# Attention: the division by the softmax sum after the values product, and masks added by VectorE in the instruction that finds the row maximum

## The chip, the cores and the metric

One core of one Trainium2 chip runs the whole program. The metric is the device time of one execution in microseconds; the time before is the median of three runs.

## The reference, cut to what matters

The program is a stack of four blocks on 512 tokens of width 1024: two "hybrid" layers, one "even" and one "odd" layer, all in float32. Most of the work is gated feed-forward matmuls. The change touches the softmax attention of three of the layers. In a hybrid layer two mixers use it, each with four heads:

```python
# mixer D (mla): plain causal attention, 4 heads, 96-dim keys, 64-dim values
logits = einsum('bthd,bshd->bhts', qb, k) * scale
logits = where(causal, logits, -inf)
p = softmax(logits, axis=-1)
out = einsum('bhts,bshd->bthd', p, v)

# mixer A (dsa): the same over the top-k keys that an indexer picks, 4 heads, 64-dim,
# with a bias by distance; unpicked keys do not count
logits = einsum('bthd,btkhd->bthk', qb, ks) * scale + bias
p = softmax(where(valid, logits, -inf), axis=-1)
out = einsum('bthk,btkhd->bthd', p, vs)
```

The even layer has 8 heads of 64 dimensions (kind E). Its three dilated branches are merged: the kernel adds ln(how many branches see this key) to the scores, with -1e30 where none does, and takes one softmax. So each of the kinds A and E has an added matrix over all its keys, while D needs one only on the diagonal block.

## The kernel before, in words

The program is written by hand, engine by engine, with counted semaphores; each engine runs its queue in program order. Activations live in SBUF with features on partitions and 512 tokens along the free axis. The eight PSUM banks hold 128x512 float32 each. Large matmuls run in three products of rounded halves (`split_product`: w_hi with hi, w_lo with hi, w_hi with lo). A weight tile of 128x1024 (a "unit") is loaded by SyncE into one of four slots; ScalarE writes `w_hi` (`split_unit`, L1379) and VectorE, sometimes GpSimd, writes `w_lo` (L1787).

Attention is a software pipeline over 32 units (`pe_attention` L1029, `act_attention` L1516, `dve_attention` L1966; `pool_attention` L2404 for A). A unit is one head and one block of 128 queries, and sees (tb + 1) x 128 keys, tb from 0 to 3. A hybrid layer does the 16 D units and then the 16 A units; the even layer 32 E units. In iteration i:

- TensorE makes the scores of unit i in one of four banks (0, 1, 4, 5): query times key (L1043, L1044), and the mask as a further matmul, identity times mask, into the same bank (L1045). For D the mask covers only the last 128 columns; for A and E it covers all keys. Then it transposes the probabilities of unit i-2, block by block (L1052, banks 2 and 3), and multiplies the values of unit i-3 (L1063): the values (128 keys x 64) are the weights, the transposed probabilities stream, and the result (64 x 128, features on partitions) lands where it belongs in bank 6 or 7, which gathers 8 units, a pair of heads.
- VectorE finds the negated maximum of unit i (L1974), takes the reciprocal of the sum of unit i-1 (L1982), multiplies the probabilities of i-1 by it (L1985), and copies the transposed probabilities of i-2 to SBUF (L1992).
- ScalarE takes the exponential of unit i from PSUM, with the maximum as bias and the sum as accumulator (L1527, two instructions). When 8 units are done it copies the gathered bank to `xn_hi` and `y` (L1533, L1534).
- For A, GpSimd adds the bias by distance to the index mask (L2413) into one of three tiles, for the mask matmul.

Beside this pipeline, ScalarE and VectorE prepare the output projection: ScalarE splits four units in iterations 12 to 15, VectorE in 15 to 18 and makes `xn_lo` tiles in 8 to 11, 13, 21 and 29. The projection `pe_out` (L858) follows directly on TensorE; `down_bank(m)` is bank (m + 6) % 8. `pe_norm` (L791) and `pe_post` (L1235) form means of squares for the norms, with separate semaphores.

Of the kernel before, what the change touches and what calls it, by code (L numbers as in the profile page):

```python
# [244 lines left out]
NORMS_POST = 3 * DEPTH + 1  # L245
Z_STAGES = [STAGES["in", _l] for _l in range(DEPTH)]
# [26 lines left out]
def program(nc, I, out):  # L273
    ctx = ExitStack()
    with ctx:
# [59 lines left out]
        def T(n):  # L335
            return arena[:, n, :]
# [37 lines left out]

        def score(tb):
            return scores[:, sc_at[tb]:sc_at[tb] + (tb + 1) * P]
# [57 lines left out]
        sq_done = sem("sq_done", 24)  # L434
        norm_ps = sem("norm_ps", 3)
        norm_ln = sem("norm_ln", 3)
        norm_r = sem("norm_r", 3)
# [72 lines left out]
        att_p = sem("att_p", 32)  # L510
# [43 lines left out]
        rsq = sem("rsq")  # L554
        rn_ps = sem("rn_ps")
        rn_ln = sem("rn_ln")
        rn_r = sem("rn_r")
# [233 lines left out]
        def pe_norm(pe, n):  # L791

            for k in range(KD):
                pe.e.wait_ge(sq_done.h, n * KD + (k + 1))
# [63 lines left out]
        def pe_out(pe, st, order, free):  # L858

            for n, k in enumerate(order):  # L860
# [4 lines left out]
                else:  # L865
                    for m in (0, 2, 3, 4, 5, 6, 7, 1):
# [162 lines left out]
        def pe_attention(pe, units, ops):  # L1029

            U = len(units)
            for i in range(U + 3):
                if i < U:
                    ops["ready"](pe, i)
                    m, h, tb = units[i]
                    if i >= 4:
                        pe.e.wait_ge(att_exp.h, att_exp.by(pe.l, i - 3))
                    s = pb[(0, 1, 4, 5)[i % 4]]
                    N = (tb + 1) * P
                    q, k = ops["qk"](m, h)  # L1040
# [14 lines left out]
                if i >= 3:  # L1055
# [17 lines left out]
        def hyb_mask(m, h, tb, u):  # L1073
            if m == "D":
                return C("causal"), tb * P
# [1423 lines left out]
```

## Time and profile before

| | us |
|---|---|
| median of 3 runs (3715.59 to 3719.69) | 3717.46 |
| profiled execution | 3722.82 |
| its span in the trace | 3721.0 |
| TensorE busy | 3533.9 (95%) |
| VectorE busy | 1606.5 (43%) |
| ScalarE busy | 1119.2 (30%) |
| GpSimd busy | 321.9 (9%) |

The span is the time from the first to the last instruction that the hardware profiler recorded. The chain of waits is followed back from the last instruction: each piece is what held up the next one. In a chain row the columns are start and length in microseconds, then engine, tile, line, and how many instructions. A float32 matmul appears as two instructions, a transpose as one. PE is TensorE's matmuls, PEld its weight loads, DVE is VectorE, ACT ScalarE, POOL GpSimd. In a timeline row the brackets hold how long the engine stood idle before the row, and what ended it.

### The profile page before, as it was taken

The page shows a single profiled execution, that of the slowest core. Times are in us where ns is not written, and L with a number is a line of the kernel's source. Part 1 is how long each engine was busy: PE and PEld are TensorE (multiplying, and loading weights), DVE is VectorE, ACT ScalarE, POOL GpSimd, SP SyncE. Part 2 cuts the span into 40 slices and gives each one's busy share as a digit, 9 for nine tenths or more (in the row PEclk, how much of TensorE's full clock was granted, in tenths as well). Part 3 has the DMA queues.
Part 4 walks back from the last instruction along what each step waited for, and adds up shares of the span by engine and source line. Part 5 has one row for each costly group of instructions (what it writes and reads, how often), then busy time and mean ns, then how long its engine had stood idle before and what let it go on. Part 6 is the DMA issues. An engine that isn't in the chain of part 4 may idle for free.

```text
span 3721.0 us, 39381 instructions
## 1 busy us (share of the span) xinstructions
PE 3533.9 (95%) x14540; PEld 2624.5 (71%) x14540; DVE 1606.5 (43%) x2252; ACT 1119.2 (30%) x1631; POOL 321.9 (9%) x180
## 2 busy tenths in 40 slices
PE   8999998999999999999899999889999998889998
PEld 5888663668887888766467888556678886568886
DVE  3332388543323332258654332734443327363322
ACT  3222334332223222234323221212232214432222
POOL 0000133100000000033210000401000002300000
PEclk9999997899999999999699999899999999899999
DMA  4332320023332333322002332331123322223332
GB/s 130 94 96 93 77 74 30 1 60 93 96 94 78 93 96 95 85 69 70 0 29 79 96 96 90 91 72 46 46 73 95 91 90 70 69 65 91 96 96 68
DMA packets 419543, 285.96 MB, mean 77 GB/s; under 512 B 57352, under 2 KB 395116, under 8 KB 419308
## 3 DMA queue, kind: packets, MB, share of 16 engines
q1 hardware_dynamic: 418624, 283.62, 26.2%
q8 instruction: 57, 0.93, 0.1%
q10 hardware_dynamic: 828, 1.13, 0.1%
q14 instruction: 34, 0.28, 0.0%
HBM read 280.24 MB, written 4.47 MB: 77 GB/s over the span
## 4 chain that ended last, share of the span: by engine, by line
PE 87%; DVE 8%; ACT 2%; issue 1%; DMA 1%; SPq 0%; POOL 0%; POOLq 0%; DVEq 0%; ACTq 0%
PE bank L800 24%; PE bank L801 23%; PE bank L802 23%; PE bank L1150 2%; PE bank L1063 1%; PE bank L795 1%; PE bank L1044 1%; PE bank L1045 1%; DVE xn_lo L1782 1%; DVE xn L1772 1%; PE bank L1144 1%; DVE arena L1881 1%; PE bank L1052 1%; DVE arena L1860 1%; DVE small L1857 1%
## 5 line engine op out<-in xcount | busy, mean ns | idle before, releaser
L802 PE MATMUL bank<-xn_lo,w_hi 128*128 128x512 f32 x2800 | 1102.1, 394 | 0.0
L800 PE MATMUL bank<-xn_hi,w_hi 128*128 128x512 f32 x2496 | 1002.2, 402 | 53.6 <-DVE xn_lo L1782 51.3
L801 PE MATMUL bank<-xn_hi,w_lo 128*128 128x512 f32 x2496 | 992.3, 398 | 0.0
L1787 DVE TENSOR_TENSOR w_lo<-wring,w_hi 128x1024 fp32r<-128x1024 f32 x434 | 537.0, 1239 | 1012.7 <-ACT w_hi L1379 995.6
L1379 ACT ACTIVATE w_hi<-wring 128x1024 fp32r<-128x1024 f32 x490 | 514.6, 1052 | 578.4 <-DMA wring<-in_ffn_down 330.2
L802 PEld LDWEIGHTS bank<-xn_lo,w_hi 128*128 128x128 f32 x2800 | 531.5, 190 | 133.5
L800 PEld LDWEIGHTS bank<-xn_hi,w_hi 128*128 128x128 f32 x2496 | 471.1, 189 | 188.8 <-issue 54.3
L801 PEld LDWEIGHTS bank<-xn_hi,w_lo 128*128 128x128 f32 x2496 | 473.3, 190 | 100.1
L801 PE MATMUL bank<-h_hi,w_lo 128*128 (+1 forms) x1056 | 419.6, 397 | 0.0
L802 PE MATMUL bank<-h_lo,w_hi 128*128 (+1 forms) x1056 | 416.5, 394 | 0.0
L800 PE MATMUL bank<-h_hi,w_hi 128*128 (+1 forms) x1056 | 415.4, 393 | 0.0
L1395 ACT ACTIVATE h_hi<-arena x132 | 83.5, 633 | 662.4 <-DVE arena L1801 662.4
L1801 DVE TENSOR_TENSOR arena<-bank,arena 128x512 f32 x132 | 91.4, 692 | 375.5 <-PE bank L802 375.5
L800 PEld LDWEIGHTS bank<-h_hi,w_hi 128*128 128x128 f32 x1056 | 198.2, 188 | 50.2
L801 PEld LDWEIGHTS bank<-h_hi,w_lo 128*128 128x128 f32 x1056 | 198.2, 188 | 47.6
L802 PEld LDWEIGHTS bank<-h_lo,w_hi 128*128 128x128 f32 x1056 | 198.2, 188 | 46.7
L2371 POOL TENSOR_TENSOR w_lo<-wring,w_hi 128x1024 fp32r<-128x1024 f32 x56 | 135.1, 2414 | 1024.8 <-ACT w_hi L1379 1024.8
L1391 ACT ACTIVATE arena<-bank 128x512 f32<-128x512 f32 x132 | 79.2, 600 | 383.9 <-PE bank L802 383.9
L1804 DVE TENSOR_TENSOR h_lo<-arena,h_hi x132 | 91.4, 693 | 134.0 <-ACT h_hi L1395 134.0
L800 PE MATMUL bank<-z_hi,w_hi 128*128 128x512 f32 (+1 forms) x304 | 127.4, 419 | 9.6 <-DVE xn_lo L1782 9.6
L801 PE MATMUL bank<-z_hi,w_lo 128*128 128x512 f32 (+1 forms) x304 | 123.3, 406 | 0.0
L1881 DVE SCALAR_TENSOR_TENSOR arena<-hpad,cur_dw,arena 128x512 f32<-128x512 f32 x120 | 111.2, 991 | 0.0
(360 smaller groups left out, 2998.4 us busy)
## 6 DMA issues: line engine op xcount, KB each, us to landing
wring<-in_ffn_gate SPq DMA_DIRECT2D x88, 512.0 KB, 3.7
wring<-in_ffn_up SPq DMA_DIRECT2D x88, 512.0 KB, 3.7
wring<-in_ffn_down SPq DMA_DIRECT2D x88, 512.0 KB, 3.5
wring<-in_ffn_w_gate SPq DMA_DIRECT2D x44, 512.0 KB, 3.7
wring<-in_ffn_w_up SPq DMA_DIRECT2D x44, 512.0 KB, 3.7
wring<-in_ffn_w_down SPq DMA_DIRECT2D x44, 512.0 KB, 3.5
wring<-in_w_in SPq DMA_DIRECT2D x34, 512.0 KB, 3.6
wring<-in_w_out SPq DMA_DIRECT2D x16, 512.0 KB, 4.9
```

The source lines that it names most:

```text
L800: nc.tensor.matmul(ps, w_hi[:, slot, t, 0:M], hi, start=start, stop=False)
L801: nc.tensor.matmul(ps, w_lo[:, slot, t, 0:M], hi, start=False, stop=False)
L802: return nc.tensor.matmul(ps, w_hi[:, slot, t, 0:M], lo, start=False, stop=stop)
L1150: mm = nc.tensor.matmul(bank[:, :], w[:, k, c * P:(c + 1) * P], xn[:, k, :], start=(k == 0), stop=(k == KD - 1))
L1379: nc.scalar.activation(w_hi[:, slot, :, :].rearrange("p k c -> p (k c)"), wunit[:, slot, :], ACT.Copy).then_inc(u_hi.h, 1)
L1391: nc.scalar.activation(sg[:, c, :], pb[c][:, :], ACT.Silu).then_inc(sg_ready.h, 1)
L1395: nc.scalar.activation(h_hi[:, bass.ds(2 * i + c, 1), :].rearrange("p a c -> p (a c)"), arena[:, bass.ds(2 * i + (H_LO + c), 1), :].rearra ...
L1787: nc.vector.tensor_tensor(w_lo[:, slot, :, :].rearrange("p k c -> p (k c)"), wunit[:, slot, :], w_hi[:, slot, :, :].rearrange("p k c -> p ...
L1801: nc.vector.tensor_tensor(h, pb[2 + c][:, :], sg[:, c, :], ALU.mult).then_inc(h_full.h, 1)
L1804: nc.vector.tensor_tensor(lo, h, hi.bitcast(F32), ALU.subtract).then_inc(h_lo_ready.h, 1)
L1881: ins = nc.vector.scalar_tensor_tensor(out=T(t_hc[ct]), in0=src, scalar=w, in1=T(t_hc[ct]), op0=ALU.mult, op1=ALU.add)
L2371: nc.gpsimd.tensor_tensor(w_lo[:, q, :, :].rearrange("p k c -> p (k c)"), wunit[:, q, :], w_hi[:, q, :, :].rearrange("p k c -> p (k c)").b ...
```

## The change

Four things change in the attention pipeline.

1. A and E: no mask matmul. VectorE reads scores and mask and writes -(scores + mask) to the probability tile, while it keeps the minimum, in one instruction; ScalarE takes exp(-x + that minimum) in place. D keeps its causal mask on TensorE and its plain reduce.
2. The multiply of the probabilities by the reciprocal is gone. The values product is turned round (transposed probabilities as weights, 64 columns of values stream), so that queries lie on partitions, and ScalarE multiplies the 128x64 result by the reciprocal on its way to SBUF (`o_buf`). The results of 8 units are then transposed, four blocks, into bank 5, from which the two copies are made.
3. Banks: scores use three (0, 1, 4); outputs alternate between 6 and 7 by unit; 5 is for the new transposes. The projection's first unit visits the banks in another order and waits for the scalings of the last two units and, for bank 5, the last copy.
4. The semaphores of `pe_norm` and `pe_post` are merged; `pe_mean` serves both.

```diff
@@ pe_attention
-            for i in range(U + 3):
+            for i in range(U + 6):
...
-                    if i >= 4:
-                        pe.e.wait_ge(att_exp.h, att_exp.by(pe.l, i - 3))
-                    s = pb[(0, 1, 4, 5)[i % 4]]
+                    if i >= 3:
+                        taken = att_exp if units[i - 3][0] == "D" else att_max
+                        pe.e.wait_ge(taken.h, taken.by(pe.l, i - 2))
+                    s = pb[(0, 1, 4)[i % 3]]
...
-                    msk, lo = ops["mask"](m, h, tb, i)
+                    lo = tb * P if m == "D" else N
                     if lo:
-                        nc.tensor.matmul(s[:, 0:lo], q[:, tb * P:N], k[:, 0:lo], start=True, stop=True)
-                    nc.tensor.matmul(s[:, lo:N], q[:, tb * P:N], k[:, lo:N], start=True, stop=False)
-                    nc.tensor.matmul(s[:, lo:N], ident, msk, start=False, stop=True).then_inc(att_s.h, 1)
+                        mm = nc.tensor.matmul(s[:, 0:lo], q[:, tb * P:N], k[:, 0:lo], start=True, stop=True)
+                    if lo < N:
+                        nc.tensor.matmul(s[:, lo:N], q[:, tb * P:N], k[:, lo:N], start=True, stop=False)
+                        mm = nc.tensor.matmul(s[:, lo:N], ident, C("causal"), start=False, stop=True)
+                    mm.then_inc(att_s.h, 1)
...
-                    pe.e.wait_ge(att_p.h, att_p.by(pe.l, u + 1))
+                    pe.e.wait_ge(att_exp.h, att_exp.by(pe.l, u + 1))
...
-                    if u % 8 == 0 and u >= 16:
-                        pe.e.wait_ge(y_att.h, y_att.by(pe.l, u // 8 - 1))
-                    o = pb[6 + (u // 8) % 2][64 * (h % 2):64 * (h % 2) + 64, tb * P:(tb + 1) * P]
+                    if u >= 2:
+                        pe.e.wait_ge(att_on.h, att_on.by(pe.l, u - 1))
+                    a = tb * P + 64 * (h % 2)
                     for b in range(tb + 1):
-                        mm = nc.tensor.matmul(o, ops["v"](m, h, b), pt_buf(units, u)[:, b * P:(b + 1) * P],
+                        mm = nc.tensor.matmul(pb[6 + u % 2][:, a:a + 64], pt_buf(units, u)[:, b * P:(b + 1) * P], ops["v"](m, h, b),
                                               start=(b == 0), stop=(b == tb))
                     mm.then_inc(att_o.h, 1)
+                u = i - 5
+                if u >= 0 and u % 8 == 7:
+                    p = u // 8
+                    pe.e.wait_ge(att_on.h, att_on.by(pe.l, u + 1))
+                    if p >= 1:
+                        pe.e.wait_ge(y_att.h, y_att.by(pe.l, p))
+                    for tb in range(TB):
+                        mm = nc.tensor.transpose(pb[5][:, tb * P:(tb + 1) * P], o_buf(units, p)[:, tb * P:(tb + 1) * P], ident)
+                    mm.then_inc(att_y.h, 1)
@@ pe_out
-                    for m in (0, 2, 3, 4, 5, 6, 7, 1):
+                    for m in (2, 3, 4, 5, 6, 0, 1, 7):
@@ att_free
             if m < 2:
-                pe.e.wait_ge(y_att.h, y_att.by(pe.l, 3 + m))
+                pe.e.wait_ge(att_on.h, att_on.by(pe.l, 31 + m))
+            elif m == 7:
+                pe.e.wait_ge(y_att.h, y_att.by(pe.l, 4))
@@ act_attention
-                    if i >= 3:
-                        act.e.wait_ge(att_t.h, att_t.by(act.l, i - 2))
...
+                    if units[i][0] == "D":
+                        if i >= 3:
+                            act.e.wait_ge(att_t.h, att_t.by(act.l, i - 2))
+                        nc.scalar.activation(p, pb[(0, 1, 4)[i % 3]][:, 0:N], ACT.Exp,
+                                             bias=nmax[:, c:c + 1], accum_out=psum_[:, c:c + 1]).then_inc(att_exp.h, 1)
+                    else:
+                        nc.scalar.activation(p, p, ACT.Exp, scale=-1.0,
+                                             bias=nmax[:, c:c + 1], accum_out=psum_[:, c:c + 1]).then_inc(att_exp.h, 1)
                 u = i - 4
+                if 0 <= u < U:
+                    _, h, tb = units[u]
+                    p = u // 8
+                    if p >= 2 and u % 8 == 0:
+                        act.e.wait_ge(att_y.h, att_y.by(act.l, p - 1))
+                    act.e.wait_ge(att_rs.h, att_rs.by(act.l, u + 1))
+                    act.e.wait_ge(att_o.h, att_o.by(act.l, u + 1))
+                    a = tb * P + 64 * (h % 2)
+                    nc.scalar.activation(o_buf(units, p)[:, a:a + 64], pb[6 + u % 2][:, a:a + 64], ACT.Identity,
+                                         scale=rsum[:, u % 4:u % 4 + 1]).then_inc(att_on.h, 1)
+                u = i - 6
                 if u >= 0 and u % 8 == 7:
-                    act.e.wait_ge(att_o.h, att_o.by(act.l, u + 1))
-                    o = pb[6 + (u // 8) % 2][:, :]
+                    act.e.wait_ge(att_y.h, att_y.by(act.l, u // 8 + 1))
+                    o = pb[5][:, :]
@@ dve_attention
+                    if m == "D":
+                        nc.vector.tensor_reduce(nmax[:, c:c + 1], s, AX.X, ALU.max, negate=True).then_inc(att_max.h, 1)
+                    else:
+                        added = mask(dve, h, tb, i)
+                        if i >= 3:
+                            dve.e.wait_ge(att_t.h, att_t.by(dve.l, i - 2))
+                        nc.vector.tensor_tensor_reduce(p_buf(units, i)[:, 0:N], s, added, -1.0, -SENTINEL,
+                                                       ALU.add, ALU.min, nmax[:, c:c + 1]).then_inc(att_max.h, 1)
...
-                        dve.e.wait_ge(att_p.h, att_p.by(dve.l, u - 3))
+                        dve.e.wait_ge(att_on.h, att_on.by(dve.l, u - 3))
                     nc.vector.reciprocal(rsum[:, c:c + 1], psum_[:, c:c + 1]).then_inc(att_rs.h, 1)
-                    p = p_buf(units, u)[:, 0:(units[u][2] + 1) * P]
-                    dve.e.wait_ge(att_rs.h, att_rs.by(dve.l, u + 1))
-                    nc.vector.tensor_scalar(p, p, rsum[:, c:c + 1], None, ALU.mult).then_inc(att_p.h, 1)
...
-                if i in (13, 21, 29):
-                    n = 4 + (i - 13) // 8
+                if i in (15, 23, 31):
+                    n = 4 + (i - 15) // 8
@@ pool_attention
-                    pool.e.wait_ge(att_s.h, att_s.by(pool.l, BM[n - 3] + 1))
+                    pool.e.wait_ge(att_max.h, att_max.by(pool.l, BM[n - 3] + 1))
```

## Rows read from the trace of the kernel before

**Rows 1.** Page, part 1: busy us (share of the span), instructions.

```profile
PE 3533.9 (95%) x14540; PEld 2624.5 (71%) x14540; DVE 1606.5 (43%) x2252; ACT 1119.2 (30%) x1631; POOL 321.9 (9%) x180
```

**Rows 2.** Chain (start, duration, what): one head of the even stage.

```profile
2606.06 0.36 PE bank L1063 x2
...
2606.84 0.42 PE bank L1045 x2
2607.26 0.45 PE bank L1052 x3
...
2612.57 1.02 PE bank L1063 x8
...
2614.64 1.06 PE bank L1045 x2
...
2615.91 0.36 PE bank L1063 x2
```

**Rows 3.** Chain of waits, kind A heads of layer 1: two multiplies.

```profile
734.14 0.74 DVE arena L1985
...
744.29 0.74 DVE arena L1985
```

**Rows 4.** Chain of waits, one D head of layer 1.

```profile
697.04 0.43 DVE arena L1985
...
699.28 0.22 PE bank L1045 x2
...
705.06 0.43 DVE arena L1985
```

**Rows 5.** Timeline (start, duration, instruction, [idle before]): D, then E head.

```profile
704.27 0.69 DVE L1974 TENSOR_REDUCE small<-bank 128x1 f32<-128x512 f32 x1 [0.60 <-PE bank L1045]
...
704.99 0.69 ACT L1527 ACTIVATE arena<-bank,small 128x512 f32<-128x512 f32 x1 [1.88 <-DVE small L1974]
...
705.54 0.31 PEld L1052 LDWEIGHTS bank<-cst,arena 128*128 128x128 f32 x3 [0.28 <-DVE arena L1985]
...
705.58 0.19 ACT L1527 ACTIVATION_READ_ACCUMULATOR arena<-bank,small 128x1 f32 x1
...
2615.73 0.69 DVE L1974 TENSOR_REDUCE small<-bank 128x1 f32<-128x512 f32 x1 [2.02 <-PE bank L1045]
...
2617.00 0.55 PE L1052 MATMUL bank<-cst,arena 128*128 128x128 f32 x3
```

**Rows 6.** Timeline, then ns min/median/max of weight loads (L1063 old values product).

```profile
2423.00 1.89 PE L1185 MATMUL bank<-arena,s_wv 128*128 128x64 f32 x16
...
2424.73 1.51 PE L1150 MATMUL bank<-xn,wring 128*128 128x512 f32 x3
...
L1185 PEld LDWEIGHTS bank<-arena,s_wv x64: 190/192/192, 2422.6 to 2452.2; 128*128 128x128 f32 x64
...
L1063 PEld LDWEIGHTS bank<-arena x480: 132/137/137, 688.3 to 2639.9; 128*64 128x64 f32 x160
```

**Rows 7.** Groups by shape: xcount | busy us, mean ns | idle before.

```profile
L1538 ACT ACTIVATE xn_hi<-xn 128x512 fp32r<-128x512 f32 x12 | 7.4, 619 | 0.0
...
L1533 ACT ACTIVATE xn_hi<-bank 128x512 fp32r<-128x512 f32 x12 | 7.1, 591 | 10.2 <-PE bank L1063 10.2
...
L1527 ACT ACTIVATE arena<-bank,small 128x128 f32<-128x128 f32 x24 | 8.9, 369 | 4.4 <-DVE small L1974 4.4
```

**Rows 8.** Page part 5, timeline, chain: head with weight splits, layer 1.

```profile
L1787 DVE TENSOR_TENSOR w_lo<-wring,w_hi 128x1024 fp32r<-128x1024 f32 x434 | 537.0, 1239 | 1012.7 <-ACT w_hi L1379 995.6
...
713.56 0.55 PE L1052 MATMUL bank<-cst,arena 128*128 128x128 f32 x3
...
724.77 0.55 PE bank L1052 x3
```

**Rows 9.** Chain of waits, end of layer 1's attention.

```profile
756.64 1.87 PE bank L1063 x14
758.51 0.44 PE bank L800
```

More of the change, by code:

```diff
@@ L245, with turn, post_turn @@
 NORMS_POST = 3 * DEPTH + 1
+def turn(n):
+    return n + max(0, n - 3 * DEPTH)
+def post_turn(m):
+    return 3 * DEPTH + 1 + 2 * m
 Z_STAGES = [STAGES["in", _l] for _l in range(DEPTH)]
@@ L373, in pt_buf, with o_buf @@
             return T(((19, 22) if units is HYB_UNITS else (37, 39))[u % 2])
+        def o_buf(units, p):
+            return T(((17, 18) if units is HYB_UNITS else (18, 19))[p % 2])
         def score(tb):
@@ L433, in program @@
         x_ready = sem("x_ready", 24)
[L434 to L437, printed above, removed]
+        sq_done = sem("sq_done")
+        norm_ps = sem("norm_ps")
+        norm_ln = sem("norm_ln")
+        norm_r = sem("norm_r")
         xn_ready = sem("xn_ready", 24)
@@ L509, in program @@
         att_rs = sem("att_rs", 32)
-        att_p = sem("att_p", 32)
+        att_on = sem("att_on", 32)
+        att_y = sem("att_y", 4)
         att_t = sem("att_t", 32)
@@ L1071, in hyb_qk, with hyb_mask, even_mask @@
             return T(t_aq[h // 2])[r:r + 64, :], T(t_ak[h // 2])[r:r + 64, :]
-        def hyb_mask(m, h, tb, u):
-            if m == "D":
-                return C("causal"), tb * P
+        def hyb_mask(dve, h, tb, u):
             if tb == 0:
-                return bias[:, h, SEQ - P:SEQ], 0
-            return T(t_bm[BM.index(u) % 3])[:, 0:(tb + 1) * P], 0
+                dve.e.wait_ge(pro_sb.h, 4 + 2 + A_HEADS)
+                return bias[:, h, SEQ - P:SEQ]
+            dve.e.wait_ge(att_bm.h, att_bm.by(dve.l, BM.index(u) + 1))
+            return T(t_bm[BM.index(u) % 3])[:, 0:(tb + 1) * P]
+        def even_mask(dve, h, tb, u):
+            return C("lnmult")[:, SEQ - (tb + 1) * P:]
         def hyb_v(m, h, b):
@@ L1121, in even_ready @@
                 eng.e.wait_ge(ez_sb.h, len(E_Z))
-        EVEN = dict(qk=even_qk, mask=lambda m, h, tb, u: (C("lnmult")[:, SEQ - (tb + 1) * P:], 0),
-                    v=lambda m, h, b: e_vv[:, b, h * E_DIM:(h + 1) * E_DIM], ready=even_ready)
+        EVEN = dict(qk=even_qk, v=lambda m, h, b: e_vv[:, b, h * E_DIM:(h + 1) * E_DIM], ready=even_ready)
         def pe_even(pe, norms):
@@ L1233, in pe_even @@
                 mm.then_inc((w_used if c else glu_ps).h, 1)
-        def pe_post(pe, m):
-            for k in range(KD):
-                pe.e.wait_ge(rsq.h, m * KD + k + 1)
-                mm = nc.tensor.matmul(pb[6][:, :], C("mean1024"), T(SQ + k), start=(k == 0), stop=(k == KD - 1))
-            mm.then_inc(rn_ps.h, 1)
         def pe_odd(pe):
@@ L1519, in act_attention @@
             U = len(units)
-            for i in range(U + 4):
+            for i in range(U + 6):
                 if i < U:
@@ L1964, in dve_mixers, with dve_attention @@
                                                in1=T(t_or[pr]), op0=ALU.mult, op1=ALU.mult).then_inc(o_n.h, 1)
-        def dve_attention(dve, units, st, order):
+        def dve_attention(dve, units, st, order, mask):
             U = len(units)
@@ L2340, in _ @@
                 dve_mixers(dve)
-                dve_attention(dve, HYB_UNITS, STAGES["out", l], Y_HYB)
+                dve_attention(dve, HYB_UNITS, STAGES["out", l], Y_HYB, hyb_mask)
                 dve_take(dve, STAGES["out", l], add)
@@ L2350, in _ @@
             dve_even(dve)
-            dve_attention(dve, E_UNITS, STAGES["out", "even"], Y_EVEN)
+            dve_attention(dve, E_UNITS, STAGES["out", "even"], Y_EVEN, even_mask)
             dve_take(dve, STAGES["out", "even"], to_r)
```

64 lines of the change are left out of this document (28 added, 36 removed).

## The prediction

> **What bounds the kernel now.** I read the page's busy table first: TensorE is busy 95% of the span, VectorE 43% [rows 1]. That is an average, so I then followed the chain of waits through the three attention stages the change touches (layer 1 from 682 to 758 us, layer 2 the same, the "even" one from 2560 to 2640). A stage has 32 units, one for each head and block of 128 queries; four units (128, 256, 384, 512 keys) make a head and the pattern repeats. In the even stage the chain of one head is TensorE and nothing else: it repeats after 2615.91 - 2606.06 = 9.85 us, four mask matmuls take 0.42 for 128 columns to 1.06 for 512, 0.21 more for each 128, so 0.42 + 0.63 + 0.84 + 1.06 = 2.95, and no wait is in it [rows 2]. Heads of kind A (layers) look alike but repeat after 744.29 - 734.14 = 10.15 us: once a head TensorE waits for the normalised probabilities, whose multiply takes 0.74 there, beside GpSimd's bias addition, where a D head shows 0.43 [rows 3, 4]. Heads of kind D repeat after 705.06 - 697.04 = 8.02 us, of which TensorE waits 0.28 for that multiply [rows 4, 5]. So TensorE is the bound and VectorE ends a wait once a head.
>
> **Sum's base.** The profiled execution took 3722.82 us (span 3721.0 plus 1.82 around it), 5.36 above the median 3717.46 of the three runs shown. Terms are worked out on the former and moved to the median.
>
> **1. Masks leave TensorE (A and E heads, 8 each; D keeps its causal mask).** Removed per head: 2.95 us [rows 2]. Not all is streaming: the mask of 128 columns costs 0.42 in an E head and 0.22 in a D head [rows 2, 4], same shape. What differs is the weights before it: 64 partitions deep in E, 96 in D. So in E a pause of 0.20 stands ahead of each mask. After the change the transposes stand behind that 64-deep matmul and probably inherit the pause. Between 0 and 0.20 for each unit comes back; I take 0.15, nearer to the mask's row because it is the same switch: +0.60 per head.
>
> **2. The values product turns round.** Weights were 64 columns of values with 128 columns of probabilities streaming; now 128 columns of transposed probabilities are weights and 64 columns stream. The state-space stage has this form: 16 such instructions from 2423.00 until the next group at 2424.73, 0.108 each [rows 6]. The old form costs (1.02 - 0.36)/6 = 0.11 each, from 8 against 2 instructions [rows 2]. So the body costs nothing more. Each group's first load stands behind a wait and is longer (190 against 137 ns by the weight-load rows [rows 6]): +0.05 a unit, +0.20 per head, all 24 heads.
>
> **3. Division after the product.** The multiply by the reciprocal (0.43 for 384 columns [rows 4]) leaves VectorE and the path from exponential to transposes. In its place ScalarE scales 128x64 out of PSUM for each unit. That form isn't in the trace; ScalarE's shortest instruction, the accumulator read of one column, takes 0.19, and its exponential of 128 columns 0.37 [rows 5, 7]: between these two, I take 0.30, as it has a scale per partition like the latter.
>
> What is late next: the product of unit u waits until unit u-2 has been scaled, since only two banks take turns. ScalarE takes the scaling of unit i-4 in order, behind the exponential of unit i. So the product of the 256-key unit waits for: widest maximum, widest exponential, accumulator read, scaling. In a D head, from the start of the widest maximum: 0.69 + 0.04 + 0.78 (exponential and its read, 704.99 to 705.77) + 0.30 + 0.05 = 1.86 us [rows 5]. TensorE would be there, without the present wait of 0.28, after 705.54 - 704.27 - 0.28 + 0.44 (transposing; 3 blocks as in rows 2) = 1.43 [rows 5]. It waits 0.43 instead of 0.28. D heads: +0.15 + 0.20 = +0.35, times 8 = +2.8 us.
>
> **4. The fused add, scale and minimum.** It replaces the reduce (0.69 at 512 columns). The trace has no such instruction. Below: the plain reduce, 0.69. Above: two full passes, 1.38. The other two-tensor form beside it, the w_lo subtraction, takes 1.24 for 1024 columns, so one pass for 512 would be under 0.7 [rows 8]. I take 0.75: one PSUM and one SBUF stream, like the reduce in length, with a little for the written tile. The exponential then reads SBUF; the same 512-column copy costs 619 ns from SBUF against 591 from PSUM [rows 7], so +0.03.
>
> The Trainium skill (VectorE: DVE Perf Modes, section "Two Vector instructions with no wait between them") says that an operation which also writes out its accumulator is two instructions. No VectorE row here shows such a pair; ScalarE's exponential does show one, 0.19 us [rows 5]. If it held, each A or E head would wait about 0.15 more (the length of a reciprocal), 2.4 us in all. The skill's same page gives ScalarE 52 cycles more for an SBUF source than for PSUM; the two copy rows show 28 ns, and the measurement decides.
>
> **A and E heads together.** From the start of the widest maximum (2615.73) to the next transposes (2617.00) TensorE needs 1.27, less a mask of 0.42, plus two pauses of 0.15, plus 0.44 for three transposes, plus 0.05: 1.64 [rows 2, 5]. The new chain: 0.75 + 0.04 + 0.81 + 0.30 + 0.05 = 1.95. Wait 0.31. Head: 9.85 - 2.95 + 0.60 + 0.20 + 0.31 = 8.01. E: 8 x (9.85 - 8.01) = 14.7 saved. A: GpSimd's addition no longer meets a multiply, so the same 8.01: 8 x (10.15 - 8.01) = 17.1 saved. Together -31.8. GpSimd must have each bias tile ready for VectorE; it works 4 units ahead on three tiles, about 3 us a head, so nothing.
>
> **5. New transposes.** Outputs now lie queries-first and are transposed back, four blocks for each pair of heads: 4 a stage. In the loop 9 times, 0.44 and a pause of 0.15: +5.4. The last of a stage stands before the output projection: TensorE waits for the last scaling (0.20 until the matmul's end is seen, 0.30, 0.05), then 0.44: about 1.0, three times: +3.0. Before, the projection followed the last product with no gap [rows 9]. The changed bank order there keeps it from waiting further: banks 0 to 4, 6 and 7 come first, 7 x 0.7 us, against two ScalarE copies of 0.6 for bank 5.
>
> **6. The stretch with weight splitting.** In four units VectorE also makes a w_lo (1.24 us) [rows 8]. New load: (0.75 + 0.15 + 0.48 for the copy, taken like the reduce at the mean length, + 1.24, with the fused instruction's mean over lengths at 0.54 instead of 0.75) = 2.41, times 4, plus one xn_lo of 0.68 now in the first of them: 10.3 us against 8.0 of TensorE. That costs 2.3 a stage. Today this head takes 724.77 - 713.56 = 11.21 against 10.15 in a layer, so 1.06 is already paid there [rows 3, 8], and none in the even stage. +2.3 + 2 x 1.2 = +4.7.
>
> **7. Semaphores of the norms merged.** Same waits, same order: nothing; no engine gets an instruction.
>
> **Sum.** -31.8 + 2.8 + 5.4 + 3.0 + 4.7 = -15.9 us. 3722.8 becomes 3706.9; on the median, **3701.6 us**.
>
> **Rivals.**
> - *Clean removal.* The transposes hide their load, the fused instruction is 0.69 and scaling 0.22, so no wait remains: a head is 9.85 - 2.95 + 0.20 = 7.1; the 16 heads save 8 x 2.75 + 8 x 3.05 = 46.4, D and transition cost 1 and 6: about -31 with the transposes, 3686 us. For it: the D head shows 96-deep weights followed without pause. Against: the 64-deep ones are not.
> - *The fused instruction is two passes.* The wait grows by 0.63 a head in 16 heads (10.1), the splitting stretch by 2.1 in three stages (6.3): -15.9 + 16.4, so about no change, 3718 us. For it: unknown instruction. Against: w_lo's rate of one pass [rows 8].
> - *Slower: the new weight loads aren't hidden.* If each of the 24 x 20 product instructions pays its load (0.190) and its streaming (0.05) one after another, 0.24 instead of 0.11, that is +0.13 x 480 = +62 us, 3764 us. It decides from 15.9 / 480 = 0.033 us an instruction. Against: 0.108 for this very shape [rows 6]. What could differ is the source, tiles that VectorE has just written.
> - *The change does not do what it says*: TensorE's masks would still be there; the diff leaves only D's, so I give it nothing.
>
> **Chances.** Forecast 0.50, clean removal 0.18, two passes 0.22, loads exposed 0.05, the rest (other stalls either way) 0.05. Differences under 0.2% (7.4 us) can't be told from none here. Faster: nearly all of the first two and a small part of the third, 0.70. Same: most of the third and the forecast's own tail, 0.20. Slower: the fourth and a bit of the third, 0.10. Range: from the clean case, 3685, to the two-pass case, 3717.
>
> **What would show it.** After: an E head's chain 8.0 us long (7.1 clean, 8.7 two passes); A the same; D 8.4. The fused row at 512 columns 0.75. Product instructions still 0.11 apart. Before one product a head TensorE idles 0.3 to 0.4 with ScalarE's scaling as releaser. A pause in PEld before the transposes in A and E, none in D. About 1 us between the last product and the projection. I am wrong if an A or E head takes over 9 us, or if the time goes to a stage outside the three.

## The result, and the profile after

| | before | after |
|---|---|---|
| median, us | 3719.69 (5 runs, 3715.59 to 3721.18) | 3743.94 (5 runs, 3717.67 to 3744.73) |
| ratio | | 1.0051 [1.0037, 1.0064] |
| profiled execution, us | 3722.82 | 3717.67 |
| mean granted clock of it | 0.960 | 0.950 |

The forecast was 3701.6 us and faster; the kernel is slower, by 0.3 to 0.5% in the two sets of runs that measured it (this one and after_again), each interval clear of 1. The executions of the changed kernel fall into two groups, 3718 to 3721 and 3736 to 3745 us (1 and 4 here, 5 and 7 of the 12 in after_again). The profile here is of the first group; one of the second stands under after_again.

The page after, part 1 and the clock row of part 2:

```profile
PE 3515.0 (95%) x14460; PEld 2639.2 (71%) x14460; DVE 1570.3 (42%) x2220; ACT 1142.2 (31%) x1727; POOL 320.4 (9%) x180
...
PEclk9999998789999999999679999999999999899999
```

TensorE has 80 instructions fewer than in [rows 1], yet is only 18.9 us less busy. The chain of one E head, the answer to [rows 2]:

```profile
2583.73 0.63 PE bank L1076 x4
...
2584.98 0.59 PE bank L1065 x4
...
2587.28 0.84 PE bank L1076 x8
...
2590.76 0.21 ACT arena L1560
...
2591.11 0.63 PE bank L1076 x4
```

It repeats after 2591.11 - 2583.73 = 7.38 us, where before it took 9.85. ScalarE's scaling (L1560) is in the chain: the new wait, 0.50 us long. A D head, for [rows 4], takes 701.67 - 694.35 = 7.32 instead of 8.02:

```profile
694.35 0.63 PE bank L1076 x4
...
697.80 0.84 PE bank L1076 x8
...
701.32 0.21 ACT arena L1560
...
701.67 0.63 PE bank L1076 x4
```

So both kinds of head gained more than forecast. The A heads, for [rows 3], are the same instructions on TensorE as the E heads:

```profile
725.48 1.60 PE bank L1076 x8
...
737.67 1.60 PE bank L1076 x8
```

They repeat after 12.19 us instead of 10.15, and TensorE doesn't wait in them: the eight product instructions take 1.60 where the E head shows 0.84. The windows tell why. Columns: busy time and instructions of each engine, then the granted TensorE clock, DMA share and GB/s. First the kernel before, then after:

```profile
720.00:740.00 20.00, 18.85 (x86) 10.55 (x85) 14.02 (x35) 5.82 (x18) 5.75 (x6) 1.00 0.00 0
740.00:760.00 20.00, 19.06 (x96) 11.49 (x95) 11.20 (x30) 5.88 (x16) 2.26 (x2) 1.00 0.00 1
```

```profile
700.00:720.00 20.00, 16.81 (x109) 12.83 (x108) 15.66 (x41) 12.87 (x36) 3.00 (x3) 0.99 0.00 1
720.00:740.00 20.00, 20.00 (x63) 13.75 (x63) 7.48 (x25) 6.10 (x20) 4.71 (x5) 0.50 0.00 1
740.00:760.00 20.00, 19.65 (x70) 13.94 (x68) 7.10 (x24) 6.24 (x20) 1.27 (x1) 0.50 0.00 0
...
2600.00:2620.00 20.00, 18.35 (x103) 12.53 (x103) 14.18 (x48) 9.89 (x35) 0.00 (x0) 1.00 0.00 0
```

In the A heads the clock is at its lower level, 1.2 of 2.4 GHz, while TensorE is busy 100%: a busy share of 1 hides that it works at half speed. Layer 2 does the same (0.50 from 1900 to 1920). The low stretch is 44 us long in layer 1, from 719.7 to 764.0, which is just behind the attention's end. What TensorE did before the fall, in the timeline of the stretch with the weight splits (for [rows 8]):

```profile
709.39 0.63 PE L1076 MATMUL bank<-arena 128*128 128x64 f32 x4 [0.57 <-ACT arena L1560]
709.95 0.70 PE L1054 MATMUL bank<-arena 64*128 64x256 f32 x2
...
711.43 0.85 PE L1076 MATMUL bank<-arena 128*128 128x64 f32 x6 [0.20 <-ACT arena L1560]
...
713.54 1.08 PE L1076 MATMUL bank<-arena 128*128 128x64 f32 x8 [0.16 <-ACT arena L1560]
...
718.89 0.63 PE L1076 MATMUL bank<-arena 128*128 128x64 f32 x4 [1.58 <-ACT arena L1560]
...
720.06 1.22 PE L1054 MATMUL bank<-arena 64*128 64x256 f32 x2
```

It waited four times, 2.51 us in all, and the next score group of 256 columns took 1.22 where the one at 709.95 took 0.70. The releaser named is ScalarE, but VectorE is what ScalarE waited for: its timeline has no gap from 709 to 718.3, with w_lo, xn_lo, fused instructions and copies. The longest wait, 1.58, stands behind a w_lo that took 1.98 us instead of 1.21, beside a GpSimd addition that began at 715.00:

```profile
715.11 1.98 DVE L1820 TENSOR_TENSOR w_lo<-wring,w_hi 128x1024 fp32r<-128x1024 f32 x1
```

Groups by shape, ScalarE in layer 1's attention, then VectorE in the even stage (for [rows 7]). L1549 is the exponential of the A heads from SBUF, L1546 that of the D heads from PSUM, L2015 the fused instruction and its accumulator read:

```profile
L1560 ACT ACTIVATE arena<-bank,small 128x64 f32<-128x64 f32 x32 | 9.6, 302 | 4.2 <-PE bank L1076 4.2
...
L1549 ACT ACTIVATE arena<-arena,small 128x512 f32<-128x512 f32 x4 | 2.9, 722 | 11.6 <-DVE small L2015 11.6
L1546 ACT ACTIVATE arena<-bank,small 128x512 f32<-128x512 f32 x4 | 2.7, 687 | 3.8 <-DVE small L2010 3.8
```

```profile
L2015 DVE CUSTOM_DVE_ANT_0 arena<-bank,cst 128x512 f32<-128x512 f32 x8 | 5.5, 690 | 7.9 <-PE bank L1054 7.9
...
L2015 DVE DVE_READ_ACCUMULATOR2_ANT small<- 128x1 f32 x32 | 2.6, 82 | 0.0
```

For [rows 6], weight loads in the E head: the pause of 0.33 stands behind the 64-deep scores, ahead of the transposes.

```profile
2584.29 0.29 PEld L1054 LDWEIGHTS bank<-arena 64*128 64x128 f32 x2
2584.91 0.42 PEld L1065 LDWEIGHTS bank<-cst,arena 128*128 128x128 f32 x4 [0.33 <-issue]
```

And the end of layer 1's attention (for [rows 9]), at half clock: 1.57 us from the last product's end (761.07) to the projection.

```profile
758.18 2.89 PE bank L1076 x14
...
761.52 1.12 PE bank L1086 x4
762.64 0.43 PE bank L810
```

To compare kernels I use two numbers from each trace. The first is the length of the three attention stages, each from its first scores to the projection's first product. The second is the **clock deficit**, the sum of (1 - granted clock) over the time, which is what full clock would have saved at most; I give it for the three stages and for the whole program.

| | layer 1, us | layer 2 | even | rest of the program |
|---|---|---|---|---|
| before | 76.5 | 76.5 | 79.9 | 3488.1 |
| after (faster group) | 82.9 | 82.8 | 62.5 | 3487.7 |
| after_again (slower group) | 84.1 | 84.1 | 80.4 | 3489.9 |

The stages together hold the differences: in the 14 profiles of this document the rest takes 3483 to 3492 us. The deficit of the rest differs more, by up to 18 us, without the time following it, so the column for the three stages is the one to read.

### The profile page after: what moved, and what is told of

Same layout as the page of the kernel before. It is cut to its first block, busy times and chain, and to the rows that moved or that the text cites. A ratio compares the mean times of both kernels' runs of the same rounds, so it can differ in the third digit from the quotient of the medians.

```text
span 3715.9 us, 39450 instructions
## 1 busy us (share of the span) xinstructions
PE 3515.0 (95%) x14460; PEld 2639.2 (71%) x14460; DVE 1570.3 (42%) x2220; ACT 1142.2 (31%) x1727; POOL 320.4 (9%) x180
## 4 chain that ended last, share of the span: by engine, by line
PE 87%; DVE 8%; ACT 2%; issue 2%; DMA 1%; SPq 0%; POOL 0%; DVEq 0%; POOLq 0%; ACTq 0%
PE bank L810 24%; PE bank L811 23%; PE bank L812 23%; PE bank L1173 2%; PE bank L805 2%; PE bank L1054 2%; PE bank L1076 2%; DVE xn_lo L1815 1%; DVE xn L1805 1%; PE bank L1065 1%; DVE arena L1914 1%; PE bank L1167 1%; DVE arena L1893 1%; DVE small L1890 1%; DVE arena L2058 0%
## 5 line engine op out<-in xcount | busy, mean ns | idle before, releaser
L810 PEld LDWEIGHTS bank<-h_hi,w_hi 128*128 128x128 f32 x1056 | 198.2, 188 | 47.5
L805 PE MATMUL bank<-arena,cst 128*128 128x512 f32 x224 | 105.9, 624 | 13.0 <-ACT arena L1368 12.5
```

The source lines that it names most:

```text
L805: mm = nc.tensor.matmul(pb[6][:, :], C("mean1024"), T(SQ + k), start=(k == 0), stop=(k == KD - 1))
L810: nc.tensor.matmul(ps, w_hi[:, slot, t, 0:M], hi, start=start, stop=False)
```

## The experiments

In the recorded expectations "head" often means a unit (units 15 to 20 and so on). Every ratio is against the kernel before, run beside it on the same chip.

| kernel | median, us | ratio, 95% interval | three stages, us | their clock deficit | whole deficit |
|---|---|---|---|---|---|
| (before) | | | 232.9 | 5.8 | 147.9 |
| (after) | | | 228.2 | 48.7 | 184.0 |
| after_again | 3738.19 | 1.0028 [1.0010, 1.0046] | 248.6 | 80.9 | 216.3 |
| filler | 3689.76 | 0.9919 [0.9907, 0.9932] | 198.5 | 7.1 | 137.3 |
| scale_first | 3729.88 | 1.0026 [1.0015, 1.0037] | 238.6 | 75.5 | 216.0 |
| masks_on_pe | 3714.41 | 0.9992 [0.9983, 1.0000] | 223.8 | 4.4 | 129.0 |
| spread_only | 3684.57 | 0.9898 [0.9883, 0.9913] | 198.9 | 17.3 | 150.4 |
| sf_spread | 3689.31 | 0.9912 [0.9898, 0.9925] | 195.9 | 28.8 | 164.1 |
| filler_stretch | 3691.47 | 0.9924 [0.9910, 0.9937] | 198.4 | 9.1 | 139.0 |
| masks_fused_only | 3766.29 | 1.0120 [1.0104, 1.0135] | 281.6 | 99.2 | 230.4 |
| before_stall | 3746.11 | 1.0071 [1.0058, 1.0085] | 256.4 | 19.2 | 155.3 |
| masks_fused_filler | 3717.97 | 0.9989 [0.9980, 0.9998] | 226.3 | 14.4 | 150.9 |
| sf_filler_stretch | 3682.69 | 0.9896 [0.9881, 0.9911] | 194.5 | 16.6 | 145.1 |
| sf_spread_filler | 3668.25 | 0.9860 [0.9845, 0.9875] | 181.9 | 6.3 | 133.1 |

The expectations quote whole deficits (148.0, 184.8, 165.4, 225.8) that were added up in windows of 20 us and only as far as 3720 us. They are within 1.3 us of the table but for masks_fused_only, whose 225.8 lacks what lies behind.

### Is it the clock, or the pipeline?

**after_again**, the changed kernel once more.

> The changed kernel once more, to see an execution of its usual time (four of five were at 3740 to 3745 us, the profiled one at 3718). Clock theory: TensorE's granted clock falls to half (1.2 GHz) in the A heads of both layers, and in the slower executions in one more stage, probably the even attention. Then the profile of an execution near 3744 us shows E heads of about 12 us at half clock, and about 25 us more lost there than in the trace at hand; median about 3744. Rival, pipeline theory: the chain through ScalarE's scaling costs more than the masks saved; then E heads at full clock take over 9 us in such an execution.

Its profile is of a 3740.3 us execution. There the even stage falls too:

```profile
2605.17 1.08 PE L1076 MATMUL bank<-arena 128*128 128x64 f32 x8 [0.16 <-ACT arena L1560]
2606.17 2.03 PE L1054 MATMUL bank<-arena 64*128 64x512 f32 x2
```

In the two profiles, one of each group, most of the difference is this one more stage at half clock: the even stage takes 80.4 instead of 62.5 us, of 22.6 in all. The waits before the fall (0.50, 0.17, 0.16) are those of the other profile (0.50, 0.18, 0.16), which kept its clock: the same program stands on an edge there. In the two layers the clock fell 8 us earlier than in the other profile, at 711.8 and 1879.2, behind waits of 0.57 and 0.20; the 1.58 wasn't needed.

**filler** adds superfluous products to TensorE, in units 15 to 20 and then in one unit of four (in the even stage in one of four from unit 4 on); their results are overwritten unread. (That is 8 units in a layer's stage and 11 in the even one; the 22 in filler_stretch's expectation is wrong.)

```diff
+                if 15 <= i < U - 1 and (units[i][2] == 0 or i <= 20) or units[0][0] == "E" and 4 <= i < U and units[i][2] == 0:
+                    n = 512 if units[i][2] == 0 else 256
+                    nc.tensor.matmul(pb[(0, 1, 4)[(i + 1) % 3]][:, 0:n], ident, C("lnmult")[:, 0:n], start=True, stop=True)
```

> Adds work that is not needed: in A and E heads one matmul of 512 columns (about 0.85 us) on TensorE into the score bank that is free next, once a head where it waits for the scaling, and 256 columns in the iterations with weight splits. Clock theory: with TensorE busy in the waits the clock stays at 2.4 GHz in the A heads, which take 7.7 to 8.2 us instead of 12.2; that saves about 33 us there and, in the slow executions, 20 to 25 more in the even stage: about 3690 us. Pipeline theory: clock or not, added work adds 0.4 us a head in 16 heads: about 3750 us.

More work, 48 us less: the granted clock is 1.00 from 700 to 760. Near the end of the even attention it still fell, behind a wait of 1.06, for 7 us (2600.0 to 2606.9).

**scale_first** moves ScalarE's scaling of unit i-4 ahead of the exponential of unit i.

```diff
@@ act_attention, ahead of the exponential
+                u = i - 4
+                if 0 <= u < U:
...
+                    nc.scalar.activation(o_buf(units, p)[:, a:a + 64], pb[6 + u % 2][:, a:a + 64], ACT.Identity,
+                                         scale=rsum[:, u % 4:u % 4 + 1]).then_inc(att_on.h, 1)
@@ and taken out behind it
-                u = i - 4
...
```

> ScalarE takes the scaling of unit i-4 ahead of the exponential of unit i, so the product no longer waits behind the widest exponential. Both theories: the waits of 0.5 to 0.67 us a head go (24 heads, 12 to 15 us at full clock). Clock theory: if that is enough to keep the clock, A heads are about 7 us at full clock and the time is about 3685 us; if the wait in the weight-split iterations alone makes the clock fall, A heads stay near 12 us and the time is about 3730. Pipeline theory: exactly the 12 to 15 us, 3730 us, with no change of clock.

The steady wait is gone, and an E head at full clock takes 2584.02 - 2577.35 = 6.67 us (chain, both rows at the head's first product):

```profile
2577.35 0.17 PE bank L1076 x2
...
2584.02 0.17 PE bank L1076 x2
```

The median, 3729.9, is the one that both theories named, so it decides nothing; the clock does. The pipeline theory said that it wouldn't change, but it falls in all three stages, in the even one at 2595.8, behind a wait of 0.60 for VectorE. The pipeline got better by 0.7 us a head and the kernel is still slower than before. So the late division's wait isn't what costs the time.

### Which part of the change, and where?

**masks_on_pe** keeps the late division; the masks are TensorE matmuls again and VectorE's reduce is plain.

```diff
@@ pe_attention
-                    lo = tb * P if m == "D" else N
+                    msk, lo = ops["mask"](m, h, tb, i)
...
-                        mm = nc.tensor.matmul(s[:, lo:N], ident, C("causal"), start=False, stop=True)
+                        mm = nc.tensor.matmul(s[:, lo:N], ident, msk, start=False, stop=True)
@@ dve_attention, and the same in act_attention
-                    if m == "D":
+                    if True:
```

> The late division and its scaling on ScalarE kept, masks of A and E back on TensorE as matmuls (and VectorE's plain maximum). Clock theory: TensorE is busy enough again and the clock stays at 2.4 GHz: A and E heads 9.2 to 9.8 us, D heads 7.3, transposes of the outputs added: about 3710 us. Pipeline theory (the late division is what costs): the wait for the scaling is still there, so at least 3740 us.

The clock holds in all three stages, though TensorE still waits 0.30 to 0.34 for the scaling in each head. An A head is 718.65 - 709.09 = 9.56 us, and the half change alone is worth nearly nothing.

**masks_fused_only** is the other half: the kernel before with the fused instruction, its early division kept.

> The kernel before with one half of the change alone: the masks are added by VectorE in the instruction that finds the maximum (in the 8 A and 8 E heads), while the division stays ahead of the values product as before. With masks_on_pe, the other half (3714.4), this tells whether the two halves add. An E head would take about 9.85 - 2.2 = 7.6 us at full clock (2.2 is what the masks cost TensorE by the E heads with and without them in masks_on_pe and in the changed kernel, 9.6 and 7.4): 16 x 2.2 = 35 us less, about 3685 us, if the clock holds. If taking the masks' columns out of TensorE is what makes the clock fall, it falls here too, in the A heads of both layers, and the time is 3715 to 3745 us. If it needs the division's waits as well, the clock holds here.

The clock fell in all three stages, as the second theory said, but the time is 21 us above its range: it is the slowest of all. VectorE now has both the fused instruction and the normalising; TensorE waited 0.53, 0.27, 0.69 and 2.29 us between 716 and 723, and the A heads then run at half clock to their end, 13.85 us each. In the even stage it fell at 2586, 5 us after the first scores and 40 us before the first w_lo of that stage (2626), and stayed low for 99 us. So other waits for VectorE than those of the split stretch can stand before a fall.

```profile
720.00:730.00 10.00, 7.71 (x25) 4.37 (x23) 6.89 (x17) 2.88 (x8) 1.99 (x2) 0.62 0.00 0
730.00:740.00 10.00, 9.61 (x28) 5.24 (x28) 5.83 (x16) 2.02 (x6) 2.26 (x2) 0.50 0.00 1
```

**masks_fused_filler** is that kernel with filler's products.

> masks_fused_only (3766.3) with the superfluous products of the run filler. If its loss against the kernel before is the clock (its sum of 1 minus the clock is 225.8 against 148.0) the time is 3766 - 78 = 3688 plus up to 10 for the products themselves: 3688 to 3700 us. If VectorE's queue of normalising and fused masks is what it loses by, it stays above 3720.

48 us come back where the clock alone would have given 78, and 3718 lies between the two forecasts (3688 to 3700, above 3720). An A head takes 9.52 us (744.43 - 734.91), of which 0.86 is filler, and a wait of 1.21 remains for VectorE's multiply, which takes 1.46 in the chain, twice what [rows 3] show; so both reasons hold in part. TensorE waited 1.85 us there as well, and the clock fell, returned after 3.5 us, and did so once more at 745.6:

```profile
720.00:730.00 10.00, 7.71 (x29) 3.87 (x27) 7.31 (x20) 2.99 (x8) 2.26 (x2) 0.83 0.00 0
730.00:740.00 10.00, 8.79 (x45) 5.04 (x45) 8.58 (x23) 3.08 (x10) 3.41 (x4) 1.00 0.00 1
```

**before_stall** makes the stretch wait in the kernel before, with nothing of the change: VectorE makes eight superfluous reductions a stage.

```diff
                 if 15 <= i < 15 + SLOTS:
+                    for n in range(2):
+                        nc.vector.tensor_reduce(spare[...], C("lnmult")[:, 0:SEQ], AX.X, ALU.max)
                     dve_units(dve, st, i - 15, i - 14)
```

> The kernel before, untouched but for eight superfluous VectorE reductions a stage (128x512, 0.69 us each, two in each of the four heads with a weight split, 1.4 us a head), so that TensorE waits longer there. All masks' products stay on TensorE and the division stays early. If TensorE's waits in the split stretch are what makes the clock fall: it falls here too, right behind the stretch, in the A heads and perhaps in the E heads, and the time is 3720 + 3 x 4.5 (the waits, VectorE being nearly full there) + 45 to 60 (what the changed kernel and masks_fused_only lost to the clock) = 3775 to 3795 us. If the fall needs the masks' columns gone or the late division, the clock holds at 1.00 in the A heads and the time is 3720 + 13 = about 3733 us.

Neither forecast is right, and this is the most telling run. The clock does fall behind the wait in all three stages, with all the masks' columns there, but it comes back after 7 to 10 us. The wait, then three windows:

```profile
725.43 0.62 PE L1053 MATMUL bank<-cst,arena 128*128 128x128 f32 x3 [2.01 <-DVE arena L1986]
```

```profile
720.00:730.00 10.00, 7.94 (x27) 4.20 (x25) 7.38 (x19) 2.87 (x9) 1.78 (x2) 0.79 0.00 0
730.00:740.00 10.00, 9.80 (x41) 5.54 (x40) 5.73 (x15) 2.38 (x8) 2.47 (x3) 0.87 0.00 1
740.00:760.00 20.00, 19.07 (x90) 10.76 (x90) 11.70 (x33) 5.36 (x16) 2.99 (x3) 1.00 0.00 1
```

So two things made the loss. A stretch in which VectorE holds TensorE up can bring the clock down, in the old kernel too. Whether it came back while the attention lasted differed with the heads that followed: with the masks' products (before_stall) or superfluous ones (masks_fused_filler) it returned, without either (after, after_again, scale_first, masks_fused_only) it stayed at half to about the attention's end.

### The stretch itself

**filler_stretch**: filler's products in units 15 to 20 alone.

```diff
+                if 15 <= i <= 20:
```

> The changed kernel with superfluous 256- or 512-column products (results overwritten, never read) in heads 15 to 20 alone, the stretch with the weight splits; filler had them in 22 heads of each stage and took 3689.8 us. If the stretch is where the clock is decided: it stays at 1.00 in the A and E heads, 3680 to 3690 us, the A heads at 7.4 us without any added work in them. If the heads after it need the added work themselves, the clock falls some heads later and the time is 3710 to 3740 us.

Nothing is added to the heads after unit 20, and in both layers they keep full clock:

```profile
720.00:740.00 20.00, 19.00 (x109) 12.85 (x107) 11.32 (x41) 10.38 (x34) 5.98 (x6) 1.00 0.01 2
740.00:760.00 20.00, 18.31 (x94) 14.74 (x93) 4.96 (x10) 4.31 (x10) 0.00 (x0) 1.00 0.16 41
```

So in the two layers the light heads didn't fall of themselves. In the even stage the clock fell at 2597.5, at the wait of 1.06 with which that attention ends, and was back at 2607.7; the same wait in the layers (742.50, 1892.98) had no fall behind it.

**spread_only** has no extra work: VectorE's four w_lo are made every fourth unit.

```diff
-                if 15 <= i < 15 + SLOTS:
-                    dve_units(dve, st, i - 15, i - 14)
+                if i in (16, 20, 24, 28):
+                    n = (16, 20, 24, 28).index(i)
+                    dve_units(dve, st, n, n + 1)
```

> The changed kernel with one edit: VectorE's four weight-split steps (w_lo), which the changed kernel does in four heads in a row, are done in every fourth head instead; the division's wait in every head (0.5 to 0.67 us) stays. If the granted clock falls because TensorE waits in the stretch with the four splits (0.57, 0.20, 0.16 and 1.58 us in the changed kernel's first stage), it stays at 1.00 in the A and E heads, the heads there take about 7.4 us instead of 12.2, and the time is about 3718 - (184.8 - 148.0) = 3681 us (184.8 and 148.0 are the sums of 1 minus the granted clock over the changed kernel and the one before). If the steady waits of every head are enough to make it fall, the A heads still take about 12 us and the time is 3718 to 3745 us. If the clock is not the cause at all, the heads at full clock change nothing and only the 1.58 us wait goes, about 5 us in three stages.

One edit of three lines turns +0.3% into -1.0%, with the steady wait (0.50) in every head: the clock is 1.00 in layer 2 and in the even stage. In layer 1 it fell late, at 731.8 us, though layer 2 shows the same waits (0.50, 0.50 and 0.15, against 0.50, 0.50 and 0.16) and kept its clock:

```profile
720.00:740.00 20.00, 19.34 (x90) 13.01 (x89) 12.82 (x40) 8.71 (x30) 5.98 (x6) 0.80 0.01 2
740.00:760.00 20.00, 19.18 (x65) 14.63 (x65) 4.93 (x14) 5.02 (x14) 0.00 (x0) 0.52 0.00 0
```

**sf_spread** is spread_only with scale_first.

> As spread_only, and ScalarE takes the scaling of head i-4 before the exponential of head i, so that the steady wait goes too. If TensorE's waits in the split stretch make the clock fall: clock 1.00 throughout, A and E heads at 6.7 us, D heads about 0.65 us shorter than in the changed kernel, 3681 - 16 x 0.7 - 8 x 0.65 = about 3665 us. If what matters is that the A and E heads have less array work than before (the masks' 512 columns are gone), the clock falls even without waits, and the time is 3700 to 3730 us as in scale_first (3729.9).

It missed by 24 us. With the A heads at 6.67 us nothing slack is left: one xn_lo that takes 1.58 instead of 0.68 beside GpSimd's addition makes TensorE wait 0.37 and 0.16, and the clock falls in both layers behind it:

```profile
724.68 0.88 PE L1076 MATMUL bank<-arena 128*128 128x64 f32 x6 [0.37 <-DVE arena L2030]
...
726.82 1.39 PE L1076 MATMUL bank<-arena 128*128 128x64 f32 x8 [0.16 <-DVE arena L2030]
728.14 2.07 PE L1054 MATMUL bank<-arena 64*128 64x512 f32 x2
```

The even stage, where GpSimd adds nothing, kept 1.00.

**sf_filler_stretch**, scale_first with filler's products in units 15 to 20:

> scale_first (3729.9) with the superfluous products in heads 15 to 20 alone. scale_first has no wait in the D and E heads and still falls to half clock behind the split stretch. If the stretch decides: the clock holds, 3691.5 (filler_stretch) - 16 x 0.7 - 8 x 0.65 = about 3675 us. If the heads without waits and without masks fall by themselves, 3700 to 3730 us.

Layer 1 and the even stage hold; in layer 2 the clock is down from 1872.1 on. Both layers show the same instructions with the same wait of 0.37, first layer 1, then layer 2:

```profile
728.82 0.88 PE L1079 MATMUL bank<-arena 128*128 128x64 f32 x6 [0.37 <-DVE arena L2033]
...
731.57 1.12 PE L1054 MATMUL bank<-arena 64*128 64x512 f32 x2
```

```profile
1869.24 0.88 PE L1079 MATMUL bank<-arena 128*128 128x64 f32 x6 [0.37 <-DVE arena L2033]
...
1871.99 2.02 PE L1054 MATMUL bank<-arena 64*128 64x512 f32 x2
```

So such a wait doesn't decide the fall alone. Against filler_stretch the kernel gained 8.8 us of the 16.4 expected (3691.5 - 3682.7).

**sf_spread_filler**, sf_spread with the products in units 21 to 24, over the place of that wait:

```diff
+                if 21 <= i <= 24:
```

> sf_spread (3689.3; weight splits every fourth head, scaling first) with superfluous products in heads 21 to 24 alone, where in sf_spread TensorE waited 0.37 and 0.16 us for VectorE (its add beside POOL took 1.58 instead of 0.68 us) and the clock then fell from 726.8 us on. If that short wait is the trigger: the clock holds, 3689.3 - (165.4 - 148) = 3672 us, with up to 5 for the added products. If not, 3685 to 3695 us.

The stretch now has no wait and the clock holds in all three stages; an A head with its new transposes takes 735.71 - 728.60 = 7.11 us. At 0.986 [0.9845, 0.9875] it beats both kernels, though it carries superfluous products in four units a stage.

```profile
720.00:730.00 10.00, 10.00 (x55) 6.99 (x55) 7.13 (x22) 4.56 (x16) 3.97 (x4) 1.00 0.01 2
```

## Why the prediction was wrong

**The failed step** is the sum's base: every term was priced at the clock that the rows of before show in these heads, 1.00, and no rival let it move. It treated 2.3 us of waits in the split stretch (step 6) as 2.3 us. They came nearly so (2.51 in layer 1), but the A heads behind them ran at 0.50 and took 12.2 - 7.4 = 4.8 us more each. The forecast's own sign of being wrong, an A head of over 9 us, came true.

What half clock cost can be read from the stages. A layer's stage takes 82.85 us in after and 66.58 in filler_stretch, which kept the clock there and carries superfluous products: about 16 us, 33 in two layers. The even stage of the slower group adds 17.9. The deficit in the three stages rose by 43 us in the faster group (48.7 - 5.8) and by 75 in the slower (80.9 - 5.8); that is more than the time lost, since at full clock part of it would have gone into the steady waits again. Against this stood 16 us forecast as gain. With the clock kept in both layers (filler, filler_stretch) the same change gives 3690 and 3691 us. That this is near the "clean removal" rival, 3686, is in part luck: that rival had no waits, and these heads have them, but their products are cheaper (steps 2 and 3 below).

The Trainium skill (TensorE: Matmul & The Clock Gate, section "A second HAM failure mode: psum-queue depth-cycling") tells of a bf16 kernel whose clock goes between its two levels, with short idle times between groups of matmuls. Here too it fell after waits of 0.16 to 2.3 us, but in the changed kernel it fell once a stage and stayed. The prediction did not draw on that page.

Step by step:

- **1, masks leave.** Right. The inherited pause shows: four transposes take 0.59 in an E head, 0.44 in a D head (+0.15 forecast).
- **2, product turned round.** Mis-sized. The body is 0.11 each as forecast ((0.84 - 0.17)/6), but the groups are shorter, not 0.05 longer: 8 instructions take 0.84 against 1.02 [rows 2], and 2 take 0.17 (scale_first) against 0.36 [rows 2]. In a D head the scores behind the product are quicker too, 0.28 against 0.42 for 128 columns. So -0.72 in an E head, and more in D, where I had +0.20.
- **3, division.** The scaling is 0.302, as estimated. The wait is 0.50 in an E and 0.57 to 0.67 in a D head against 0.31 and 0.43, since TensorE gets there sooner. It costs more than it lasts, 7.38 - 6.67 = 0.71 us an E head (scale_first), because the product behind it takes 0.63 instead of 0.41. D heads: 7.32 against a forecast of 8.4 and 8.02 before.
- **4, fused instruction.** 0.690 at 512 columns (0.75 forecast): one pass. Its accumulator read is a second instruction of 82 ns, as the Trainium skill says (VectorE: DVE Perf Modes, "Two Vector instructions with no wait between them"); the estimate of 0.15 a head was too long, and its piece of the chain is 0.09 to 0.10. The exponential from SBUF costs 35 ns more than from PSUM (722 against 687), near the 28 of the copies.
- **A and E together.** An E head 7.38 against 8.01. The terms add up: 9.85 - 2.95 (masks) + 0.48 (pauses, three of 0.15 and one of 0.03) - 0.72 (products) + 0.71 (wait) = 7.37. The rival "two passes" falls with 0.690, "loads exposed" with 0.11 an instruction.
- **5, new transposes.** 0.44 to 0.45 each time at full clock; at the end 1.57 at half clock where I had 1.0.
- **6, split stretch.** The waits came nearly as sized. In the sum each w_lo takes 1.24; one took 1.98, beside GpSimd's addition. What the waits set off is the failed step above.
- **7, semaphores.** The rest of the program takes 3487.7 us against 3488.1, which fits the forecast of nothing; no run takes this edit alone.

The forecast's own sum from measured heads, 8 x (9.85 - 7.38) + 8 x (10.15 - 7.38) + 8 x (8.02 - 7.32) = 47.5 saved, less the new transposes and the stretch (about 13), is -34: 3683 on the median of before. The two runs with the clock kept in the layers come within 9 us of it and carry superfluous products. The same sum with half clock added, -34 + 33 = -1 and -34 + 51 = +17, is near what the two groups show against before, -2 and +22.

**What stays open.** That the half clock is what the change loses by is shown. That waits of the split stretch set it off is shown by before_stall, which adds only VectorE work that makes TensorE wait there, and fell in all three stages; filler_stretch and spread_only fit, but the first also adds work and the second still fell in layer 1. Waits don't settle it alone: the same ones kept or lost the clock in two layers (spread_only, sf_filler_stretch), in two executions (after, after_again), and masks_on_pe waits in every head and kept it. Why the clock returned in some kernels and not in others is shown only in part: with the masks' products and superfluous ones it did, but streamed columns, rows of weights and TensorE's waits changed together in these runs. Nor is the steady wait cleared: spread_only fell late in layer 1 with it, and sf_spread fell without it.

## What to carry to other kernels

Price each stage at the clock that it will have, not that of before: when an edit takes work off TensorE and leaves a neighbour engine full, look for the stretch where TensorE begins to wait, and read the granted clock behind it, in more than one execution. A busy share of 100% with instructions of twice their length is the sign. Before giving up a change that loses this way, spread the neighbour's burst: three lines on VectorE's side took the ratio from 1.0028 to 0.9898 here, some 48 us.

## What the runs showed of the hardware

- Half clock outlasted the waits before it: in after it lasted from 720 us to 764, just behind the attention's end, in before_stall 7 to 10 us. Waits of 0.37 and 0.16 us, after 15 us without any, were followed by a fall in both layers of sf_spread; a wait of 0.37 was followed by one in layer 2 of sf_filler_stretch and not in layer 1.
- Added work can shorten a program: superfluous products took the changed kernel from 3738 (after_again) to 3690 us (filler).
- In the chain, a group of 64-column products with 128x128 weights is 0.17 to 0.19 us shorter than one of as many 128-column products with 128x64 weights (0.17 and 0.36 for two instructions, 0.84 and 1.02 for eight).
- VectorE's fused instruction with one input in PSUM and one in SBUF took 0.690 us for 128x512, the length of the plain reduce, and its accumulator read 0.082 more.
- VectorE's 128x512 subtraction from SBUF took 1.58 us beside a GpSimd addition, 0.68 without (sf_spread); the 128x1024 one 1.98 against 1.21 (after).
